# Trainium2 kernel study: late modulation vectors as VectorE dot products, gate/up tiles as three 256-column products

## The reference, cut to what matters

```python
def second_block(x, c, ada_w, ada_b, norm_gain, ffn_w_gate, ffn_w_up, ffn_w_down, ...):
    c_act = jax.nn.silu(c)                                  # (1, 1024)
    for i in range(4):
        mod = c_act @ ada_w[i] + ada_b[i]                   # (1, 6 * 1024)
        sh1, sc1, g1, sh2, sc2, g2 = [m[:, None, :] for m in jnp.split(mod, 6, axis=-1)]
        h = modulate(rms_norm_2(x, norm_gain[i, 0]), sh1, sc1)
        y = attention_i(h)          # stick-breaking, MoBA, sliding window, stick-breaking
        x = x + g1 * y
        h = modulate(rms_norm_2(x, norm_gain[i, 1]), sh2, sc2)
        x = x + g2 * swiglu(h, ffn_w_gate[i], ffn_w_up[i], ffn_w_down[i])
    return x

def swiglu(h, w_gate, w_up, w_down):
    return (jax.nn.silu(h @ w_gate) * (h @ w_up)) @ w_down  # inner width 2816
```

## Time and profile before

| | |
|---|---|
| runs, median (lowest to highest) | 1978.79 us (1975.87 to 1979.99) |
| profiled execution, span from first to last instruction | 1974.8 us |
| TensorE / VectorE / ScalarE / GpSimd busy | 91% / 59% / 41% / 4% |
| mean granted TensorE clock | 0.971 |
| bytes moved | 550.35 MB, mean 279 GB/s |

### The profile page before, as it was taken

One profiled execution on the slowest core, in us unless ns is written; L12 is line 12 of the kernel. 1 busy time (PEld: TensorE's weight loads), 2 busy tenths in 40 slices (PEclk: granted clock), 3 DMA queues, 4 the chain that ended last, 5 costly groups with the idle time before them and its releaser, 6 DMA issues.

```text
span 1974.8 us, 33559 instructions
## 1 busy us (share of the span) xinstructions
PE 1789.4 (91%) x14042; PEld 1434.3 (73%) x14042; DVE 1161.9 (59%) x1929; ACT 800.8 (41%) x1344; POOL 72.8 (4%) x131
## 2 busy tenths in 40 slices
PE   6999876776776899999999899999999999989998
PEld 4897634433443688888888788887688888978887
DVE  1885101101101587787768788765788776777774
ACT  2575100000000466545445554534554444755443
POOL 0200000000000001000000000000000000000000
PEclk9999899889889899999999999999999999999999
DMA  9788999999999957744773574566475478333533
GB/s 403 281 295 326 415 428 429 428 428 429 428 428 429 396 214 303 295 180 179 301 299 129 214 299 170 221 258 256 160 294 187 147 306 335 129 115 144 199 137 132
DMA packets 43774, 550.35 MB, mean 279 GB/s; under 512 B 6673, under 2 KB 7057, under 8 KB 9233
## 3 DMA queue, kind: packets, MB, share of 16 engines
q1 hardware_dynamic: 34992, 452.13, 57.8%
q0 software_dynamic: 8672, 96.67, 11.8%
HBM read 547.53 MB, written 1.05 MB: 278 GB/s over the span
## 4 chain that ended last, share of the span: by engine, by line
PE 68%; DMA 21%; DVE 7%; ACT 2%; issue 1%; SPq 0%; DVEq 0%; ACTq 0%
PE bank L649 25%; DMA ada_ring<-in_moe_side 16%; PE bank L644 14%; PE bank L650 13%; PE bank L946 3%; PE bank L718 2%; PE bank L629 1%; DMA ring<-in_v 1%; DMA ring<-in_moe 1%; DMA ada_ring<-in_ada_last 1%; PE bank L1233 1%; PE bank L1101 1%; PE bank L1086 1%; DMA ring<-in_down 1%; DVE acts L2637 1%
## 5 line engine op out<-in xcount | busy, mean ns | idle before, releaser
L650 PE MATMUL bank<-acts,ring_parts 128*128 128x256 f32 x2248 | 631.6, 281 | 0.0
L650 PEld LDWEIGHTS bank<-acts,ring_parts 128*128 128x128 f32 x2248 | 425.3, 189 | 0.0
L649 PE MATMUL bank<-acts,mixT_parts 128*128 128x512 f32 x1096 | 390.4, 398 | 3.8 <-DVE ring_parts L2592 3.3
L649 PE MATMUL bank<-acts,xn_parts 128*128 128x512 f32 x736 | 262.0, 398 | 0.0
L649 PEld LDWEIGHTS bank<-acts,mixT_parts 128*128 128x128 f32 x1096 | 205.9, 188 | 57.2 <-DVE ring_parts L2592 6.3
L1382 ACT CAST mixT_parts<-ring 128x1024 fp32r<-128x1024 f32 (+1 forms) x152 | 152.4, 1005 | 202.0 <-PE bank L650 185.0
L2256 DVE TENSOR_TENSOR mixT<-mixT,bank 128x128 f32<-128x128 f32 x32 | 9.2, 288 | 334.2 <-ACT mixT L1591 334.2
L644 PE MATMUL bank<-acts,ring_parts 128*128 128x256 f32 x600 | 168.8, 281 | 0.0
L1382 ACT CAST xn_parts<-ring 128x1024 fp32r<-128x1024 f32 x106 | 110.6, 1053 | 142.8 <-PE bank L650 141.9
L649 PEld LDWEIGHTS bank<-acts,xn_parts 128*128 128x128 f32 x736 | 138.3, 188 | 34.4
L2594 DVE TENSOR_TENSOR ring_parts<-ring,mixT_parts 128x1024 fp32r<-128x1024 f32 x88 | 107.6, 1224 | 30.3 <-ACT mixT_parts L1382 30.3
(11 more groups left out here) (385 smaller groups left out, 3205.6 us busy)
## 6 DMA issues: line engine op xcount, KB each, us to landing
ring<-in_moe SPq DMA_DIRECT2D x48, 2048.0 KB, 27.2
ada_ring<-in_moe_side SPq DMA_DIRECT2D x48, 2048.0 KB, 25.9
ada_ring<-in_ada POOLq DMA_DIRECT2D x45, 2048.0 KB, 13.1
ring<-in_gu SPq DMA_DIRECT2D x44, 2048.0 KB, 8.1
ring<-in_down SPq DMA_DIRECT2D x32, 1408.0 KB, 6.2
ring<-in_qk SPq DMA_DIRECT2D x12, 2048.0 KB, 9.0
ring<-in_out SPq DMA_DIRECT2D x9, 2048.0 KB, 8.0
ring<-in_na SPq DMA_DIRECT2D x8, 2048.0 KB, 8.6
```

The costliest lines, as they stand in the source:

```text
L649: mm(dst[:, :], w[0], both(*x), start=start, stop=False)
L650: return mm(dst[:, 0:T], w[1], x[0], start=False, stop=stop)
```

## The change

For layers 1 to 3, chunks 0 to 8 of the modulation weights are laid out transposed. VectorE multiplies each 1024-element row with silu(c) and sums it in one instruction (`dots`, 36 per layer: three behind each of gate/up steps 1 to 10 of the layer before and two behind each of down steps 1 to 3), then adds the bias (`take_dots`). The row of silu(c) is made once: GpSimd spreads it, TensorE broadcasts it with two matmuls in the gap before layer 0's gate/up, ScalarE copies it. The groups "ffn", "down" and, from layer 1 on, "attn" disappear with their loads' users on TensorE, their copies on ScalarE, their turns and their `take_mods`. The "pairs" group stays. Gate/up tiles become `split_product`s, two tiles to a bank, four banks in turn; ScalarE takes the silu straight from PSUM and VectorE's product reads the up tiles from PSUM; `gather_halves` disappears. Some of VectorE's orders change: fewer `add_squares` ahead of the last update, `take_mods` of the "pairs" group behind it. The vectors of odd layers live in another tile. The renaming of one semaphore and a pad tile are left out below.

```diff
-            for g in range(1, 4 * LAYERS):
-                for m in chunks_of(g + 1) if g + 1 < 4 * LAYERS else ():
+            for g in range(1, PAIRED):
+                for m in chunks_of(g + 1):
                     chunk(m)
                 turn(g)
+            pool.wait_ge(x_done, KT * 2 + 2)
+            nc.gpsimd.tensor_tensor(c2_spread.rearrange("p (k n) -> p k n", k=KT), cst("ident").unsqueeze(1).broadcast_to([P, KT, P]),
+                                    c2_wide[:, :, 0:1].broadcast_to([P, KT, P]), ALU.mult).then_inc(pool_made, 1)
+            for i in layers:
+                if i + 1 in layers:
+                    for m in range(12 * (i + 1), 12 * (i + 1) + 3):
+                        chunk(m)
+                turn(paired(i))
+                if i + 1 in layers:
+                    for m in range(12 * (i + 1) + 3, 12 * (i + 2)):
+                        chunk(m)
...
-                    if i + 1 in layers:
-                        pe.wait_ge(x_done, KT * (2 + 2 * i) + 4)
-                        group_rows(group_of(i + 1, 0), "ffn", 0, 1)
+                    if i == 0:
+                        pe.wait_ge(pool_made, 3)
+                        pe.wait_ge(x_done, KT * 2 + 4)
+                        for c in range(2):
+                            m = mm(bank[6 + c][:, :], cst("ones"), c2_spread[:, 512 * c:512 * (c + 1)], start=True, stop=True)
+                        m.then_inc(row_made, 1)
                     norm_of_sums(5 + 2 * i)
-                    if i + 1 in layers:
-                        group_rows(group_of(i + 1, 0), "ffn", 1)
...
-                    def gate_up(step, r):
+                    def gate_up(step):
                         n = n0 + step
                         for f in range(2 if step == 0 else 0, 4):
-                            if step > 0:
-                                pe.wait_ge(gu_sum, 4 * (GU * i + step - 1) + f + 1 + 4 * RING * r)
-                            pe.wait_ge(w_lo, 4 * split_count(i, step) + f + 1 + 4 * RING * r)
+                            if step > 1 and f == 0:
+                                pe.wait_ge(ffn_silu, GU * i + step - 1)
+                            elif step > 1 and f == 2:
+                                pe.wait_ge(ffn_hid, GU * i + step - 1)
+                            pe.wait_ge(w_lo, 4 * split_count(i, step) + f + 1)
                             for k in range(KT):
-                                m = wide_product(bank[f], (part["whi"][f][:, k, :], part["w_gu"](n, f)[:, k, :]),
-                                                 (part["xsq"][:, k, :], part["hT"][:, k, :]), k == 0, k == KT - 1)
+                                m = split_product(gu_tile(step, f), (part["whi"][f][:, k, :], part["w_gu"](n, f)[:, k, :]),
+                                                  (part["xsq"][:, k, :], part["hT"][:, k, :]), k == 0, k == KT - 1, True)
                             m.then_inc(tile_done if f < 3 else used[n % RING], 1)
...
                     first_gate_up()
-                    for step in range(RING):
-                        gate_up(step, 0)
-                    steps(pe, RING, GU, gate_up)
-                    if i + 1 in layers:
-                        pe.wait_ge(gu_sum, 4 * (GU * i + GU - 1) + 1)
-                        pe.wait_ge(ada_taken, group_of(i + 1, 1))
-                        group_rows(group_of(i + 1, 1), "down")
+                    for step in range(GU):
+                        gate_up(step)
...
-                def silu(step, r):
-                    s = step % RING
-                    act.wait_ge(gu_sum, 4 * (GU * i + step) + 2 + 4 * RING * r)
-                    A(gact[s][:, :, :], gact[s][:, :, :], ACT.Silu).then_inc(ffn_silu, 1)
...
                 split(0, 0, 3)
-                if i + 1 in layers:
-                    group_out(group_of(i + 1, 0), "ffn")
+                if i == 0:
+                    act.wait_ge(row_made, 1)
+                    for c in range(2):
+                        m = copy(c2_row[:, 512 * c:512 * (c + 1)], bank[6 + c][:, :])
+                    m.then_inc(row_taken, 1)
                 silu_tables()
...
+            def dots(i, d0, d1):
+                mod = mods(i)
+                for d in range(d0, d1):
+                    m, q = 12 * i + d // 4, d % 4
+                    if q == 0:
+                        wait_ada(dve, m)
+                    w = ada_buffer(m)[:, q * D:(q + 1) * D]
+                    r = V.tensor_tensor_reduce(w, w, c2_row[:, :], 1.0, 0.0, ALU.mult, ALU.add, mod[:, d:d + 1])
+                    if q == 3:
+                        r.then_inc(ada_used, 1)
+            def take_dots(i):
+                mod, n = mods(i), 4 * DOTTED
+                dve.wait_ge(ada_used, ada_place(12 * i + DOTTED - 1) + 1)
+                then(V.tensor_tensor(mod[:, 0:n], mod[:, 0:n], vc("b_ada2", MODS * i, n), ALU.add), "mods")
+                V.scalar_tensor_tensor(gain[:, 0, :], mod[:, KT:2 * KT], 1.0, vc("gains2", 2 * i * KT, KT), ALU.add, ALU.mult).then_inc(mods_ready, 1)
...
                 for c in range(2):
                     for f in range(4):
-                        if (c, f) == (1, 3):
-                            take_mods(group_of(i, 3))
                         update(c, f, FIRST[f"out_{i + 1}"] + c, 1 + i, 2)
                         if c == 0:
                             low_out(1, f)
+                        if (c, f) == (1, 0):
+                            add_squares(5 + 2 * i, 1, 4)
                         if (c, f) == (1, 1):
                             first_low(0)
-                            add_squares(5 + 2 * i, 1, 4)
+                            add_squares(5 + 2 * i, 4, 5)
                         if (c, f) == (1, 2):
                             first_low(1)
-                            add_squares(5 + 2 * i, 4, KT - 1)
+                            add_squares(5 + 2 * i, 5, 6)
+                add_squares(5 + 2 * i, 6, KT - 1)
+                take_mods(paired(i))
...
-                def gather_halves(step, f):
-                    if f < 3:
-                        dve.wait_ge(tile_done, 3 * split_count(i, step) + (2 if step == 0 and f == 0 else f + 1))
-                    else:
-                        wait_used(dve, FIRST[f"gu_{i}"] + step)
-                    V.tensor_reduce(gact[step % RING][:, f, :] if f < 2 else hid[:, 2 * step + f - 2, :],
-                                    bank[f][:, :].rearrange("p (n t) -> p t n", n=2), AX.X, ALU.add).then_inc(gu_sum, 1)
                 def product(step):
                     dve.wait_ge(ffn_silu, GU * i + step + 1)
-                    dve.wait_ge(gu_sum, 4 * (GU * i + step + 1))
-                    two = hid[:, 2 * step:2 * step + 2, :]
-                    V.tensor_tensor(two, gact[step % RING][:, :, :], two, ALU.mult).then_inc(ffn_hid, 1)
+                    wait_used(dve, FIRST[f"gu_{i}"] + step)
+                    V.tensor_tensor(hid[:, 2 * step:2 * step + 2, :], gact[step % RING][:, :, :], pair_of(bank[step % 2 * 2 + 1]), ALU.mult).then_inc(ffn_hid, 1)
                 def gate_up(step):
                     for f in range(4):
-                        gather_halves(step - 1, f)
                         split(step, 0, f)
                     product(step - 1)
-                if i + 1 in layers:
-                    split(0, 0, 2)
-                normalise_split(5 + 2 * i, split_norms(i, True), 2, 3 * KT)
-                if i + 1 not in layers:
-                    split(0, 0, 2)
+                normalise_split(5 + 2 * i, split_norms(i, True), 2, mods(i), 3 * KT)
+                split(0, 0, 2)
                 split(0, 0, 3)
-                for step in range(1, RING):
+                if i == 0:
+                    dve.wait_ge(row_taken, 1)
+                for step in range(1, GU):
                     gate_up(step)
-                    if step == 2 and i + 1 in layers:
-                        take_mods(group_of(i + 1, 0))
-                for step in range(RING, GU):
-                    gate_up(step)
-                    if i + 1 in layers and step < RING + 6:
-                        half = (step - RING) % 2
-                        sum_chunk(12 * (i + 1) + 3 + (step - RING) // 2, 4 * half, 4 * half + 4)
+                    if i + 1 in layers:
+                        dots(i + 1, 3 * (step - 1), 3 * step)
...
-                for f in range(3):
-                    gather_halves(GU - 1, f)
-                    hidden(f)
-                gather_halves(GU - 1, 3)
+                for p in range(3):
+                    hidden(p)
                 split(0, 0, 0, True)
                 product(GU - 1)
...
                 for step in range(1, KT):
                     down(step, 0)
-                    if i + 1 in layers and step in (4, 5):
-                        sum_chunk(12 * (i + 1) + 8, 4 * (step - 4), 4 * (step - 4) + 4)
+                    if i + 1 in layers and step in (1, 2, 3):
+                        dots(i + 1, 28 + 2 * step, 30 + 2 * step)
```

(14 more changed lines are left out.)

177 lines of the change are left out of this document (88 added, 89 removed).

## The result

Four runs of the changed kernel took 1992.02 to 1994.14 us, median 1993.37; beside them the kernel before took 1978.72 (median of four). The ratio is 1.0077, 95% interval 1.0061 to 1.0093: slower by 14.7 us. The forecast was slower by 4.3, 1983.1 us, and its range ended at 1991. The direction was right, the time is 2.4 us outside the range. The profiled span went from 1974.8 to 1990.2 us, the mean granted clock from 0.971 to 0.964.

What follows compares the result with a forecast made beforehand. TensorE bounds the phases, the norm's chain the gaps between. Layer 0 +11.0, layers 1 and 2 +1.1, layer 3 -0.5, gate/up to down -6.4, attention gaps -0.3, down chunk -0.6: together +4.3, median 1983.1 us, range 1972 to 1991.

Steps and rivals of the forecast that it cites:

- layer 0's turn: Gap before layer 0's gate/up: small transfers behind three chunks in GpSimd's queue land late, delaying TensorE: +8.4 us.
- the landing: Layer 0's last half of the pairs transfers arrives at 812.5, between 807 and 816: -5 to +4 us around the forecast.
- the clock: Emptied gaps lower TensorE's clock behind them: +1.56 us per gate/up phase in layers 0 to 2, +3.9 us before attention.
- Rival (a): Layer 0's turn lands in time, so layer 0 behaves as layer 1: in all -5.4, median 1973.4 us; chance 0.12.
- Gate/up as three products: In each gate/up phase three products take 0.357 us against 0.354: +1.1 us per layer, 0 to +3.
- Rival (b): The gaps before gate/up and attention don't lower the clock: -10.1 us, median 1973.0 us; chance 0.11.
- Gaps and down: Start 4.85 us behind the last matmul before gate/up, saving 2.1 (layer 3: 1.55); first down step 1.6 us earlier per layer.
- the down chunk of layer 1: In layer 1's down phase, modulation chunks no longer start beside one exposed chunk landing: -0.6 us.
- The gaps before attention: Ahead of layers 1 to 3's attention the norm's chain starts earlier: -1.3 us, layer 2 -1.6, in all -4.2.
- The dots at nothing: VectorE's dots behind gate/up steps cost nothing, as the next low part has 2.5 us of slack per step.
- Rival (c): VectorE is late: dots hold a split up by 1 us in each of 30 steps, +30, 2013 us; chance 0.09.
- (d): Removed modulation products come off TensorE's path one for one in gaps and before down: -32, 1947 us; chance 0.05.

Runs made afterwards that it cites:

- split_only: The kernel before with only gate/up as three 256-column products and no gathers, modulation left on TensorE: 1981.54 us, ratio 1.0019.
- the fill: Small products of constants, read by nobody, put in the gaps of the changed kernel with layer 0's turn moved first: 1968.17 us, ratio 0.9954.
- wide_gu: Changed kernel with turn first and gaps filled, gate/up put back to 512- and 256-column products with gathers, dots kept: 1962.26 us, ratio 0.9924.
- wide_2dots_again: Second execution of the code with turn first, gaps filled, product pair back, two dots per gate/up step, down's low part ahead of two gathers: ratio 0.9909.

## Why the prediction was right in direction and wrong in size

Two terms of the sum were mis-sized, both too low: layer 0's turn, +8.4 forecast and +12.55 measured, and the product in four layers, +4.4 forecast and +9.3 measured. And the range left one of them out: it added up the bounds of the landing (-5 to +4) and of the clock (-3 to +3), but not the product's own 0 to +3 per layer, which alone reach 7.6 us above the forecast.

*Layer 0's turn*, the term that decides, was right in mechanism: the turn was late, VectorE stood in `take_mods`, and TensorE started 2.53 us behind the landing (2.4 forecast). Its size was off by 4.15 us, +12.55 instead of +8.4. I let the last half land at 812.5 inside 807 to 816; it landed at 817.8, outside my own bounds. Three parts add to 5.3: the second update ended 1.4 us later with everything ahead of it (the gap too began 1.2 us later, so only 0.2 of this counts in its length), the spread took 2.82 us and not the 1.9 of a row with another operand (0.9), and from the first chunk's issue to the last half's landing it took 28.1 us and not 25.1. The small transfers land right behind the chunk that stands ahead of them, so the third chunk's landing, 26.3 us behind its issue, was the term to look for; my bounds held the 28.1 us (20 to 29) but began 2.3 us early, at 787.4 where the first chunk is issued at 789.6. The rule of the Trainium skill that the forecast weighed ("DMA: Bandwidth & Descriptors", section "Queues, rings and completion order") holds in these traces: 25.1 us behind three chunks, 20.3 behind two, 6.5 with none ahead and three behind. The page states the ring order in its paragraph on the queues of SyncE and ScalarE; that GpSimd's queue keeps it is what these runs add. Rival (a) is refuted. Its price doesn't come out either: with the turn in time it had 1973.4, and the three kernels that have it so took 1978.5 to 1980.8. The product's 4.9 us are most of what is missing.

*Gate/up as three products* is the other mis-sized term: +1.1 per layer forecast, +2.3 measured (`split_only`), in four layers 4.9 us. The step that failed here is the reading of a pitch. I took 0.357 from 66 matmuls in 7.85 us and 0.354 from the whole phase of 352. Both ratios are too rough for a term of 0.003 times 352: one is 66 matmuls with an end effect, the other has the slower start in it. The starts in windows of steady state give 0.3600 and 0.3533, twice the difference. My bounds, 0 to +3, did hold it.

*The clock* was right in its sum: 1.56 per gate/up phase of layers 0 to 2 forecast, 1.5 measured (128.4 less 126.92), and layer 3, which had it already, lengthened by the product alone, 126.16 to 128.45. What I read off layer 3 as the clock holds 0.3 us of the slower start; the clock itself is 1.2. Ahead of attention I charged all three gaps 1.3, together 3.9. Layers 1 and 3 had 2.2 and 2.3 us, with a whole 5 us at the lower level in the windows. Layer 2 had none and ran 1.2 shorter, and not by the change as far as is known: the kernel before has a stretch at the lower level in the midst of this attention (0.59 from 1409.5 to 1413.7), the changed kernel has none there. The sum, 3.3, came out near by luck. Rival (b) is refuted by the windows and by the fill. The rule of the Trainium skill that spoke against the change ("TensorE: Matmul & The Clock Gate", section "HAM oscillation — how this bites in real kernels") agrees with six of the seven gaps of this execution and with 37 of 42 in all; the gap of 3.98 us, with 1.00 behind it here, goes either way.

*Gaps and down* were right to 0.1 us: 4.85 before gate/up (three times 4.85 or 4.86), and behind gate/up -7.1 against -7.0 with the down chunk of layer 1. The gaps before attention gave 1.20 each where I had 1.3 to 1.6.

*The dots at nothing* was right, and by more than I allowed: no TensorE wait inside gate/up, and in `wide_gu` VectorE carried 23 us more. Rival (c) is refuted. So is (d): TensorE's products were in the shadow of the norm.

The remaining 2.4 us of the profiled pair are scatter of the first block and of the tail. By the medians the gap between forecast and result is 10.3 us, of which turn and product are 9.1.

The change holds a gain that it gives away. By medians, in us, each of its own series with the kernel before at 1977.1 to 1978.7: 1993.4 as it is, 1980.8 with the turn first, 1968.2 with the gaps filled, 1962.3 with the product pair back, 1956.4 with the dots spread and the low part ahead. The last is 1.0% under the kernel before (0.8 to 1.3%; 0.9% in its second series), with the modulation on VectorE and without the new gate/up.

## What to carry to other kernels

When an instruction moves into a queue, list what the queue then holds ahead of each small transfer that somebody waits for: here 3 KB behind three 2 MB chunks of the same queue landed in 25 us, and in 6.5 with the chunks behind it. When work leaves TensorE from a gap whose length another chain sets, the time of that work doesn't come back, and the clock behind the gap can fall to its lower level; here a few products that nobody reads, put into these gaps, gave back about 10 us. A term that is a small difference of pitches times hundreds must be read from starts in steady state, and its bounds belong into the range. An engine's load must be summed over the phase that its slack covers, not over a step.

## What the runs showed that I had not expected

A 512-column and a 256-column product as a pair have two steady pitches at the full clock, and each of the 24 profiled phases of this form keeps one of them from its first to its last step. Windows of 100 us inside two gate/up phases of one execution, `wide_2dots_again`, layers 0 and 1:

```profile
820.00:920.00 100.00, 100.00 (x568) 86.76 (x567) 90.42 (x118) 43.01 (x45) 2.12 (x4) 1.00 0.72 267
1150.00:1250.00 100.00, 100.00 (x578) 87.41 (x578) 91.71 (x118) 43.60 (x45) 2.16 (x4) 1.00 0.72 267
```

568 against 578 matmuls in the same time: 0.3533 us and 0.3467 per pair, 2.25 us per phase. The same code had its four phases at 122.70, 122.72, 124.97 and 122.71 us in one execution and at 124.95, 122.72, 124.95 and 124.95 in the next, so the pitch is settled anew each time. The fill doesn't decide it: without fill, layer 2 had the faster one, and with it eight phases of 16 had. In the kernel before all four profiled phases had the slower one, and the three-product form had 0.3600 in every phase of every run. What settles the pitch stays open; it was not tried.

The spread on GpSimd took 2.82 us for 128x1024 elements where the nearest row, with one operand of another kind, had 1.90.
